# VectorE's expert loop cut to one head per pass, ScalarE's order in the memory stage, and chunk 1's output product finished ahead of its transpositions

## The chip, the cores and the metric

The kernel is one program on one core of a Trainium2 chip. The metric is the device time of one execution in microseconds (us); the number that counts is the median over the runs. TensorE (PE) multiplies matrices and transposes, VectorE (DVE), ScalarE (ACT) and GpSimd (POOL) work on tiles, and SyncE (SP) issues the ordinary loads. GpSimd issues the gathers. The engines run side by side and wait for each other through semaphores.

## The reference, cut to what matters

One layer over 256 tokens of width 1024, all in float32: a norm, one wide projection, then three branches (causal attention with rotary positions, a gated delta rule, and attention over 256 memory tokens), mixed by sigmoid gates and projected back; then a product-key expert layer.

```python
h = rms_norm(x, attn_norm_g); proj = h @ w_in
moba_out, dn_out = attention(8 heads), gated_delta_rule(8 heads) * silu(z)
mem_out = softmax(cq ck^T / 16) cv                     # 4 heads of 256
mixed = sum_n sigmoid(gate_n) * (branch_n @ w_branch[n])
x = x + mixed @ w_out
h2 = rms_norm(x, ffn_norm_g); q = h2 @ w_q             # 8 heads, two halves
experts, sc = top 16 of (top16(q1 keys1) + top16(q2 keys2))     # per token, per head
x = x + sum_k softmax(sc)_k * gelu(h2 . u[e_k]) * v[e_k]
```

The expert layer reads, for each of 256 tokens and 8 heads, 16 rows of 2048 floats (u and v of one expert lie side by side): 256 gathers of 1 MB.

## The kernel before

Each engine has its own program, written out by hand, and the order of that text is the order in which the engine works. Tokens are two chunks of 128 (c = 0, 1).

**Projection stages.** Weights come as tiles of 512 KB through a ring of three buffers (`raw` and `halves`, index i % 3). `load` (SP) fills `raw`, `high` (ACT, L555) writes a rounded copy, `low` (POOL, L918) the rest of it, and PE multiplies both (L1450 to L1452, 24 products a tile). `high` of a tile waits until PE is done with the tile three before it (`before`, `tiles_done`), `load` until that tile's `low` is done. The stages are "mv", "lead", "kv", seven times "head", "last", three times "mem", "mlast", "branch". While PE multiplies tiles, the small steps of a head lie between them: `fill(n)` puts n eighths of tiles ahead of the next small step.

**Memory stage.** `mem_head(m)` for m = 0 to 3. ACT turns the sums of squares into inverse roots (L769 to L775: Ln, then Exp), DVE scales query and key with them (L1195), PE makes the scores (L1708), ACT and DVE the softmax, PE turns it (L1715, event `p_turned`), ACT copies it out of PSUM (L558, `pT_ready`), and PE multiplies by the values (L1723). ACT also does for the next memory head: the copy of values (`take_mem_values`), squares and Silu of the delta rule's branch (`dn_head_squares`, L635 and L636), and at m = 0 the Sigmoid of the first eight gate tiles (L810). A change of function on ACT takes an ACT_TABLE_LOAD.

**Output and first routing.** PE makes `output(c, n)` (L1747, 16 pieces of products in two halves n), DVE adds it to x (`add_x1`, L1361), PE transposes it (`turn_x1`, L1756), DVE scales the transpose (`turned_x1`, L1367), and PE makes queries (L1762) and scores (L1769) of `first_head(c)`. DVE then finds the top 16 (`whole_route`). For chunk 1, DVE does in turn add_x1(1,0), turned_x1(1,0), add_x1(1,1), turned_x1(1,1), the norm and the routing, and only then its first expert row.

**Expert loop.** For each unit (head h, chunk c) GpSimd gathers 16 rows into a ring of 8 (`rows_uv`, L967); DVE takes the dot product with h2 (L1316), ACT the gelu (L859), DVE multiplies by the softmax weight (`coefficients`, L1324), ACT makes a diagonal matrix (L863), PE adds the row (L1799) and gives the ring slot back (`vrow`). Between its dots DVE routes the next head (`route_steps`). DVE's program has the bodies of heads 0 and 1 written out, a loop over j with two bodies (L1402, two passes: heads 2 to 5), and heads 6 and 7 written out. ACT and PE have a loop of two bodies with three passes (L907, L1837), GpSimd one unit pair a pass. The weights lie in four tiles `wts[par][c]`.

## Time and the profile before

| what | value |
|---|---|
| median of 3 runs | 1276.69 us (1274.66 to 1276.82) |
| profiled execution | 1273.94 us, its span 1272.1 us, mean clock 0.983 |
| PE busy | 1108.5 us, 87% of the span |
| DVE / ACT / POOL busy | 709.0 / 521.9 / 614.0 us |
| gathers | 268.45 MB of 355.32 MB moved |

The span runs from the first to the last instruction; 1.84 us of the profiled execution lie outside it. The profiled execution is 2.75 us faster than the median. Busy shares are means over stages with different limits, so they say little by themselves.

### The profile page before, as it was taken

How to read it: one execution, taken by the hardware profiler on the slowest of the kernel's cores; microseconds unless marked ns; L12 is line 12 of the kernel's file. 1: busy time of each engine (PE TensorE's matmuls, PEld its weight loads, DVE VectorE, ACT ScalarE, POOL GpSimd, SP SyncE). 2: the span in 40 equal slices, each digit the busy share in tenths (PEclk: the TensorE clock that was granted, in tenths of full speed). 3: DMA queues.
4: the chain of work that ended last, by engine and by line, in shares of the span. 5: the costliest groups of instructions: out<-in, count | busy, mean ns of one | idle time of the engine just before them, and what ended most of it. 6: DMA issues, size and time to landing. Idle time of an engine off the chain costs nothing.

```text
span 1272.1 us, 17107 instructions
## 1 busy us (share of the span) xinstructions
PE 1108.5 (87%) x5387; PEld 764.2 (60%) x5387; DVE 709.0 (56%) x1691; ACT 521.9 (41%) x1036; POOL 614.0 (48%) x447
## 2 busy tenths in 40 slices
PE   5989999999999999999888797797977978977776
PEld 5869999999998899885434252342523524422222
DVE  4535555554543332335766767666756666676554
ACT  4555566555565776512332223332333132321211
POOL 2376766567674666752234334343444434444331
PEclk8999999999999999999899999999989999999999
DMA  7453443343444453975799999999989999999996
GB/s 247 121 170 85 114 117 105 105 118 99 116 107 110 133 137 110 297 253 215 303 423 405 421 409 423 422 407 421 400 353 419 410 423 422 402 422 420 421 422 262
DMA packets 161377, 355.32 MB, mean 279 GB/s; under 512 B 7983, under 2 KB 123182, under 8 KB 127406
## 3 DMA queue, kind: packets, MB, share of 16 engines
q0 software_dynamic: 36864, 268.45, 51.3%
q1 hardware_dynamic: 124462, 86.27, 22.9%
q8 instruction: 22, 0.36, 0.1%
q14 instruction: 29, 0.24, 0.0%
HBM read 353.65 MB, written 1.05 MB: 279 GB/s over the span
## 4 chain that ended last, share of the span: by engine, by line
PE 49%; DMA 29%; issue 8%; ACT 6%; DVE 4%; POOL 4%; POOLq 0%; DVEq 0%; ACTq 0%; SPq 0%
DMA top<-peer_uv_dram,route 21%; PE ps L1799 13%; PE ps L1450 6%; PE ps L1451 6%; PE ps L1452 6%; DMA front<-peer_uv_dram,route 5%; PE ps L1762 4%; POOL split L918 2%; PE ps L1747 2%; PE ps L1610 2%; ACT split L555 2%; DMA front<-in_w_branch_dram 2%; PE ps L1629 2%; PE ps L1628 1%; ACT top L863 1%
## 5 line engine op out<-in xcount | busy, mean ns | idle before, releaser
L1799 PE MATMUL ps<-top 128*128 128x512 f32 x640 | 306.2, 619 | 91.6 <-ACT top L863 91.5
L918 POOL TENSOR_TENSOR split<-front,split 128x1024 fp32r<-128x1024 f32 x123 | 296.8, 2424 | 183.9 <-ACT split L555 183.7
L967 POOL DMA_INDIRECT top<-peer_uv_dram,route x160 | 166.0, 1038 | 261.0 <-PE ps L1799 253.5
L1799 PEld LDWEIGHTS ps<-top 128*128 128x128 f32 x640 | 118.8, 195 | 264.8 <-ACT top L863 149.7
L1316 DVE CUSTOM_DVE_ANT_0 top<-top,scratch 128x1024 f32<-128x1024 f32 x160 | 196.1, 1226 | 144.1 <-DMA top<-peer_uv_dram,route 144.1
L1450 PE MATMUL ps<-split 128*128 128x256 f32 (+1 forms) x768 | 241.4, 314 | 9.3 <-POOL split L918 5.0
L1451 PE MATMUL ps<-split 128*128 128x256 f32 (+1 forms) x768 | 225.1, 293 | 0.0
L1452 PE MATMUL ps<-split 128*128 128x256 f32 (+1 forms) x768 | 224.8, 293 | 0.0
L863 ACT ACTIVATE top<-cst,route 128x128 f32<-128x128 f32 x256 | 88.7, 393 | 280.9 <-DVE route L1324 277.5
L555 ACT ACTIVATE split<-front 128x1024 fp32r<-128x1024 f32 x128 | 133.7, 1056 | 140.6 <-PE ps L1452 85.9
L1450 PEld LDWEIGHTS ps<-split 128*128 128x128 f32 x768 | 147.1, 192 | 16.6 <-issue 8.4
L1799 PE MATMUL ps<-front,top 128*128 128x512 f32 x256 | 126.3, 617 | 34.9 <-ACT top L863 34.9
L1451 PEld LDWEIGHTS ps<-split 128*128 128x128 f32 x768 | 147.3, 192 | 3.8 <-issue 1.0
L1452 PEld LDWEIGHTS ps<-split 128*128 128x128 f32 x768 | 146.8, 191 | 2.9
L967 POOL DMA_INDIRECT front<-peer_uv_dram,route x64 | 66.9, 1045 | 136.4 <-PE ps L1799 94.6
L1799 PEld LDWEIGHTS ps<-front,top 128*128 128x128 f32 x256 | 47.7, 194 | 106.4 <-ACT top L863 55.0
L1316 DVE CUSTOM_DVE_ANT_0 front<-front,scratch 128x1024 f32<-128x1024 f32 x64 | 78.6, 1227 | 40.1 <-DMA front<-peer_uv_dram,route 32.8
L859 ACT ACTIVATE route<-route 128x2 f32<-128x2 f32 x128 | 26.0, 203 | 147.5 <-DVE route L1316 147.1
L1799 PE MATMUL ps<-scratch,top 128*128 128x512 f32 x128 | 61.0, 599 | 0.0
L1762 PE MATMUL ps<-scratch,branch_part 128*128 128x256 f32 (+1 forms) x288 | 58.5, 357 | 1.6 <-DVE scratch L1367 1.6
L1762 PEld LDWEIGHTS ps<-scratch,branch_part 128*128 128x128 f32 x288 | 50.2, 190 | 14.3 <-issue 7.2
L1450 PE MATMUL ps<-branch_hi,split 128*128 128x256 f32 x192 | 55.5, 289 | 1.5 <-POOL split L918 1.3
(263 smaller groups left out, 1594.3 us busy)
## 6 DMA issues: line engine op xcount, KB each, us to landing
front<-in_w_in_dram SPq DMA_DIRECT2D x88, 512.0 KB, 3.8
front<-in_w_branch_dram SPq DMA_DIRECT2D x24, 512.0 KB, 4.9
front<-in_w_mem_kv_dram SPq DMA_DIRECT2D x16, 512.0 KB, 3.9
top<-in_w_out_dram SPq DMA_DIRECT2D x8, 512.0 KB, 6.6
rest<-peer_w_q_by_head_dram SPq DMA_DIRECT2D x3, 1024.0 KB, 9.0
gate_part<-peer_w_q_by_head_dram SPq DMA_DIRECT2D x3, 1024.0 KB, 14.8
top<-peer_uv_dram,route POOLq DMA_INDIRECT x160, 10.3
branch_part<-peer_w_q_by_head_dram SPq DMA_DIRECT2D x2, 1024.0 KB, 6.1
```

The lines of the kernel that those rows point to most:

```text
L555: act.activation(halves[i % 3][:, 0], raw[i % 3], ACT.Copy).then_inc(hi_ready, 1)
L859: act.activation(gelu[c][:, a:b], acts[c][:, a:b], ACT.Gelu_apprx_tanh).then_inc(names["gelu"].sem, 1)
L863: act.activation(diag[:, k % 8, :], ident, ACT.Copy, scale=coef[c][:, k:k + 1]).then_inc(names["diag"].sem, 1)
L918: pool.tensor_tensor(halves[i % 3][:, 1], raw[i % 3], halves[i % 3][:, 0], ALU.subtract).then_inc(lo_ready, 1)
L967: pool.indirect_dma_start(rows_uv[k % RING], None, peer_uv, bass.IndirectOffsetOnAxis(ap=idx[c][:, k:k + 1], axis=0)).then_inc(s_row[k % R ...
L1316: dve.tensor_tensor_reduce(out=row, in0=row, in1=h2[:, c, :], scale=1.0, scalar=0.0, op0=ALU.mult, op1=ALU.add, accum_out=acts[c][:, k:k + ...
L1450: pe.matmul(dst, lhs[0], rhs[0], start=first, stop=False)
L1451: pe.matmul(dst, lhs[0], rhs[1], start=False, stop=False)
L1452: return pe.matmul(dst, lhs[1], rhs[0], start=False, stop=last)
L1610: ins = pe.matmul(ps[:, 4, a:b], BT[:, s, a:b], X[:, a:b], start=True, stop=True)
L1762: ins = pe.matmul(ps[:, 6 + i, a:b], wq[par][:, k, i * P:(i + 1) * P], h2T[:, k, a:b], start=(k == 0), stop=(k == KT - 1))
L1799: ins = pe.matmul(ps[:, 2 * c + half, :], diag[:, k % 8, :], rows_uv[k % RING][:, D + half * 512:D + (half + 1) * 512], start=False, stop= ...
```

## The change

It has four edits.

1. **DVE's expert loop.** The four weight tiles become one range, and `wts(par, c, a, b)` picks a part of it by an address that may hold a loop variable. Head 0 is written out, heads 1 to 6 are a loop in a loop (`j` and `par`) with one body, head 7 is written out. The parity of the heads is swapped.
2. **ACT ahead of the head loop.** The copies of `memv[0]` out of PSUM stand behind the first `high` of "head" and no longer behind the second.
3. **ACT in the memory stage.** The Sigmoid of gates 0 to 7 moves from memory head 0 into the last head, ahead of the wait for `dn_out`. `take_mem_values(0)` and the Silu `silu_z(0)` move behind the three `high` of memory head 0. The copy for `pT_ready` moves ahead of `high(tile 5)`, and in the last memory head ahead of the first "branch" `high` and the gate copy.
4. **PE.** `output(1, 1)` no longer has `turn_x1(1, 0)` between its sixth and seventh step; the transpositions follow it.

```diff
-        wts = [[small_of(TOPK) for _ in range(NC)] for _ in range(2)]
+        AT_WTS = at_route[0]
+        small_of(2 * NC * TOPK)
+        def wts(par, c, a=0, b=TOPK):
+            return route[:, bass.ds(par * (NC * TOPK) + (AT_WTS + c * TOPK + a), b - a)]
...
-            for i in range(2):
-                high("head", 0, i)
+            high("head", 0, 0)
             act.wait_ge(tiles_done, made("kv", 0, 7))
             for n in (1, 0):
                 act.activation(memv[0][:, n * 512:(n + 1) * 512], ps[:, 3 + n, :], ACT.Copy).then_inc(memv_kept, 1)
-            high("head", 0, 2)
+            for i in range(1, 3):
+                high("head", 0, i)
...
                 if last:
                     evacuate_mem(0, 1, kind)
+                    for gate in ("gate0", "gate1"):
+                        act.wait_ge(names[gate].sem, 1 + KT // 2)
+                    act.activation(gates[:, 0:8, :], gates[:, 0:8, :], ACT.Sigmoid).then_inc(names["sig"].sem, 1)
...
                 if last:
-                    act.wait_ge(names["vtok_kept"].sem, HEADS)
-                    take_mem_values(0)
                     dn_head_squares(0)
...
                 high(*of_head(h + 1, 1))
                 high(*of_head(h + 1, 2))
+                if last:
+                    act.wait_ge(names["vtok_kept"].sem, HEADS)
+                    take_mem_values(0)
+                    silu_z(0)
...
+                if not last:
+                    high(*tile(4))
+                    evacuate_mem(m + 1, 0, kind)
+                on(act, "p_turned", it)
+                copy("pT_ready", mpT, ps[:, 5, :])
                 if last:
                     high("branch", 0, 0)
                     act.wait_ge(tiles_done, made(*kind, 1))
                     copy("gate0", gates[:, 16 + 2 * m:18 + 2 * m, :], two(ps[:, 7, :]))
-                else:
-                    high(*tile(4))
-                    evacuate_mem(m + 1, 0, kind)
-                    high(*tile(5))
-                on(act, "p_turned", it)
-                copy("pT_ready", mpT, ps[:, 5, :])
...
-                    if m == 0:
-                        act.activation(gates[:, 0:8, :], gates[:, 0:8, :], ACT.Sigmoid).then_inc(names["sig"].sem, 1)
+                    silu_z(m + 1)
...
-            body_dve(0, 0, True, True)
-            body_dve(1, 1, True)
-            with dve.Fori(1, (PHEADS - 2) // 2) as j:
-                for par in range(2):
-                    body_dve(j * 2 + par, par, True)
-            body_dve(PHEADS - 2, 0, True)
-            body_dve(PHEADS - 1, 1, False)
+            body_dve(0, 1, True, True)
+            with dve.Fori(0, (PHEADS - 2) // 2) as j:
+                with dve.Fori(0, 2) as par:
+                    body_dve(j * 2 + par + 1, par, True)
+            body_dve(PHEADS - 1, 0, False)
...
-            output(1, 1, turn=(1, 0))
+            output(1, 1)
             pe.sem_inc(done("vrow"), PRIME)
+            turn_x1(1, 0)
             first_head(1)
```

On DVE, at the entry of the loop of the kernel before: the branch, and then the first rows of head 2. ISA rows of L1322 and L1323 are register steps, those of L1316 the dots.

```order
L1298 TENSOR_REDUCE route<-scratch 128x32
L1301 SCALAR_TENSOR_TENSOR route<-route 128x16
L1402 UNCONDITIONAL_BRANCH
L1402 ISA
L1316 ISA front,route<-front,scratch 128x1024
L1316 ISA route 128x1
L1322 ISA
L1323 ISA
L1324 TENSOR_TENSOR route<-route 128x2
```

The end of the new loop on DVE, with the two jumps back (L1414 the inner, L1413 the outer loop), followed by the first row of head 7.

```order
L1310 TENSOR_REDUCE route<-scratch 128x32
L1264 REGISTER_ALU
L1313 SCALAR_TENSOR_TENSOR route<-route 128x16
L1414 REGISTER_ALU
L1414 COMPARE_AND_BRANCH
L1413 REGISTER_ALU
L1413 COMPARE_AND_BRANCH
L1328 ISA front,route<-front,scratch 128x1024
```

In this listing the loop of before has 358 rows from its first to its jump, the new inner loop 197, ACT's loop (L907, the same before and now) 227. Each `coefficients` in the new loop has one register row more (of L1336) than before.

On ACT, from the last head into memory head 0, before: L558 of branch_part is `dn_kept`, the next two are `take_mem_values(0)`, L636 is the Silu, L555 the three `high` of memory head 0, L769 the start of the inverse roots.

```order
L558 ACTIVATE branch_part<-ps 128x256
L558 ACTIVATE scratch<-top 128x256
L558 ACTIVATE scratch<-memv 128x256
L635 ACTIVATE scratch<-branch_part 128x512
L636 ACT_TABLE_LOAD
L636 ACTIVATE scratch<-front 128x512
L558 ACTIVATE front<-ps 128x256
L558 ACTIVATE gate_part<-ps 128x256
L555 ACTIVATE split<-front 128x1024
L558 ACTIVATE gate_part<-ps 128x256
L555 ACTIVATE split<-front 128x1024 x2
L769 ACT_TABLE_LOAD
```

The same place on ACT of the changed kernel (L746 is the Sigmoid, L645 the Silu, L561 `high`; the row after these is L783, the former L769).

```order
L746 ACTIVATE gate_part<-gate_part 128x2048
L564 ACTIVATE branch_part<-ps 128x256
L641 ACTIVATE scratch<-branch_part 128x512
L564 ACTIVATE front<-ps 128x256
L564 ACTIVATE gate_part<-ps 128x256
L561 ACTIVATE split<-front 128x1024
L564 ACTIVATE gate_part<-ps 128x256
L561 ACTIVATE split<-front 128x1024 x2
L564 ACTIVATE scratch<-top 128x256
L564 ACTIVATE scratch<-memv 128x256
L645 ACT_TABLE_LOAD
L645 ACTIVATE scratch<-front 128x512
```

The two copies, the table load and the Silu stood ahead of the three `high` and now stand between them and the inverse roots.

On PE, chunk 1's output and first queries, before and then now (L1747/L1757 the output product, L1756/L1766 `turn_x1`, L1762/L1772 the queries).

```order
L1747 MATMUL ps<-top,front 128x512 x14
L1756 MATMUL ps<-cst,branch_part 128x128 x4
L1747 MATMUL ps<-top,front 128x512 x2
L1762 MATMUL ps<-scratch,branch_part 128x128 x8
L1756 MATMUL ps<-cst,branch_part 128x128 x4
```

```order
L1757 MATMUL ps<-top,front 128x512 x16
L1766 MATMUL ps<-cst,branch_part 128x128 x4
L1772 MATMUL ps<-scratch,branch_part 128x128 x8
L1766 MATMUL ps<-cst,branch_part 128x128 x4
```

The first four transpositions now stand directly ahead of the queries that need them.

## Rows read from the trace of the kernel before

**Rows 1.** The page, part 2: GB/s in 40 slices of 31.8 us.
```profile
GB/s 247 121 170 85 114 117 105 105 118 99 116 107 110 133 137 110 297 253 215 303 423 405 421 409 423 422 407 421 400 353 419 410 423 422 402 422 420 421 422 262
```

**Rows 2.** Chain that ended last: start us, us; first query of one head.
```profile
662.30 3.45 PE ps L1762 x16
...
905.99 3.45 PE ps L1762 x16
...
990.98 3.45 PE ps L1762 x16
```

**Rows 3.** Timeline of DVE at the end of head 3; idle time in brackets.
```profile
936.23 0.17 DVE L1301 SCALAR_TENSOR_TENSOR route<-route 128x16 uint32<-128x16 f32 x1
941.96 1.22 DVE L1316 CUSTOM_DVE_ANT_0 front<-front,scratch 128x1024 f32<-128x1024 f32 x1 [5.55 <-issue]
```

**Rows 4.** Line L1402, window 930 to 945: duration ns, first and last start us.
```profile
L1402 DVEq COMPARE_BRANCH  x1: 62/62/62, 936.3 to 936.3; - x1
L1402 DVEq FUSED_REGOPS  x1: 93/93/93, 941.8 to 941.8; - x1
```

**Rows 5.** Line L907, window 943 to 945: ACT's own jump back.
```profile
L907 ACTq COMPARE_BRANCH  x1: 45/45/45, 943.7 to 943.7; - x1
L907 ACTq FUSED_REGOPS  x1: 68/68/68, 943.9 to 943.9; - x1
```

**Rows 6.** Timelines of DVE, ACT and PE ahead of the head loop.
```profile
90.91 1.29 DVE L1183 COPY memv<-ps 128x512 f32<-128x512 f32 x2 [11.06 <-PE ps L1452]
...
92.07 1.06 ACT L555 ACTIVATE split<-front 128x1024 fp32r<-128x1024 f32 x1 [2.50 <-DMA front<-in_w_in_dram]
93.03 1.07 ACT L703 ACTIVATE top<-ps 128x512 f32<-128x512 f32 x2
...
94.44 1.10 PE L1585 MATMUL ps<-rest 128*128 128x512 f32 x2 [3.56 <-ACT top L703]
```

**Rows 7.** Timelines of ACT, PE and DVE, last head into memory head 0.
```profile
396.15 0.39 ACT L558 ACTIVATE branch_part<-ps 128x256 f32<-128x256 f32 x1 [6.43 <-PE ps L1650]
396.43 0.41 ACT L558 ACTIVATE scratch<-top 128x256 f32<-128x256 f32 x1
...
397.68 1.28 ACT L636 ACT_TABLE_LOAD   x1
...
399.51 0.37 ACT L558 ACTIVATE front<-ps 128x256 f32<-128x256 f32 x1
...
403.28 1.28 ACT L769 ACT_TABLE_LOAD   x1
...
399.19 1.89 PE L1695 MATMUL ps<-scratch,cst 128*128 128x256 f32 x8
...
407.82 1.52 DVE L1195 TENSOR_TENSOR scratch<-scratch 128x1024 f32<-128x1024 f32 x1 [12.68 <-ACT scratch L773]
```

**Rows 8.** Chain that ended last: memory head 0's scores.
```profile
409.66 1.74 PE ps L1708 x8
```

**Rows 9.** PE's waits, 395 to 565 us: us in total, times, longest.
```profile
PE ps L1723 <- ACT scratch L558: 4.2, 4, 2.1
```

**Rows 10.** Timeline of PE: the start of memory head 1, and of "branch".
```profile
436.10 0.39 PE L1450 MATMUL ps<-split 128*128 128x256 f32 x1 [1.67 <-POOL split L918]
...
514.96 0.47 PE L1450 MATMUL ps<-branch_hi,split 128*128 128x256 f32 x1
```

**Rows 11.** Timeline of ACT: `high` of the fourth "branch" tile, after the Sigmoids.
```profile
519.08 1.04 ACT L555 ACTIVATE split<-front 128x1024 fp32r<-128x1024 f32 x1
```

**Rows 12.** Chain that ended last: output and first queries of chunk 1.
```profile
596.77 0.44 PE ps L1756 x4
597.21 1.72 PE ps L1747 x4
...
601.18 0.70 DVE scratch L1367
```

**Rows 13.** Timeline of POOL: the ninth gather.
```profile
624.42 1.12 POOL L967 DMA_INDIRECT front<-peer_uv_dram,route  x1 [18.50 <-PE ps L1799]
```

More of the change, by code:

```diff
@@ L635, in dn_head_squares, with silu_z @@
                 act.activation(two(sqd), branch[:, 8 + 2 * m:10 + 2 * m, :], ACT.Square).then_inc(names["dn_sq"].sem, 1)
+            def silu_z(m):
                 act.activation(two(zs), zT[:, 2 * m:2 * m + 2, :], ACT.Silu).then_inc(names["z_silu"].sem, 1)
@@ L790, in mem_head @@
                     copy("gate0", gates[:, 16 + 2 * m:18 + 2 * m, :], two(ps[:, 7, :]))
-                else:
-                    high(*tile(4))
-                    evacuate_mem(m + 1, 0, kind)
-                    high(*tile(5))
-                on(act, "p_turned", it)
-                copy("pT_ready", mpT, ps[:, 5, :])
-                if last:
                     high("branch", 0, 1)
@@ L800, in mem_head @@
                 else:
+                    high(*tile(5))
                     high(*tile(6))
@@ L1303, in route_steps, with weigh @@
                 assert step[0] == RSTEPS
-            def weigh(n, out):
+            def weigh(n, par, c):
                 on(dve, "exps", n)
@@ L1309, in weigh @@
                 dve.wait_ge(done("weighed"), n * 2 + 1)
-                dve.tensor_scalar(out, ex, rsum[:, 0:1], None, ALU.mult).then_inc(done("weighed"), 1)
+                dve.tensor_scalar(wts(par, c), ex, rsum[:, 0:1], None, ALU.mult).then_inc(done("weighed"), 1)
             def dot(n, c, k):
@@ L1323, in coefficients @@
                 dve.wait_ge(done("gelu"), n * NG + (g + 1))
-                dve.tensor_tensor(coef[c][:, a:b], gelu[c][:, a:b], weights[:, a:b], ALU.mult).then_inc(done("coef"), 1)
+                dve.tensor_tensor(coef[c][:, a:b], gelu[c][:, a:b], wts(weights, c, a, b), ALU.mult).then_inc(done("coef"), 1)
             def add_out(c):
@@ L1332, in unit_dve @@
             def unit_dve(n, c, par, steps, first=False, last=False):
-                before_w, after_w = (wts[par][0], wts[1 - par][0]) if c else (wts[1 - par][1], wts[par][1])
+                other = par * -1 + 1
                 for k in range(TOPK):
@@ L1338, in unit_dve @@
                     if k == 0 and not first:
-                        coefficients(n - 1, 1 - c, NG - 1, before_w)
+                        coefficients(n - 1, 1 - c, NG - 1, par if c else other)
                     elif k and k % GROUP == 0:
-                        coefficients(n, c, k // GROUP - 1, wts[par][c])
+                        coefficients(n, c, k // GROUP - 1, par)
                     if k == 7 and not first and not last:
-                        weigh(n + 1, after_w)
+                        weigh(n + 1, other if c else par, 1 - c)
                     if k == 12 and last:
@@ L1394, in _ @@
             norm_dve(1)
-            weigh(0, wts[0][0])
+            weigh(0, 1, 0)
             whole_route(1, 1)
-            weigh(1, wts[0][1])
+            weigh(1, 1, 1)
             for c in range(NC):
                 dve.wait_ge(t_h2[c], 4)
-            body_dve(0, 0, True, True)
-            body_dve(1, 1, True)
-            with dve.Fori(1, (PHEADS - 2) // 2) as j:
-                for par in range(2):
-                    body_dve(j * 2 + par, par, True)
-            body_dve(PHEADS - 2, 0, True)
-            body_dve(PHEADS - 1, 1, False)
-            coefficients(UNITS - 1, 1, NG - 1, wts[1][1])
+            body_dve(0, 1, True, True)
[3 more added lines that the diff above has]
+            body_dve(PHEADS - 1, 0, False)
+            coefficients(UNITS - 1, 1, NG - 1, 0)
             add_out(1)
```

## The prediction, on record before the run

> **What bounds the kernel now.** I read the bytes moved per slice first. Up to slice 16 the rates are mostly between 85 and 250 GB/s, and PE has hardly a pause there. From slice 21 on they stay at about 420 GB/s, with one slice at 353 [rows 1]. So there are two regimes. Up to about 560 us PE sets the time, and only what ends one of its waits can count. In the expert loop the gathers set it, and only what leaves them without work counts. Between the two, from 565 to 620 us, lies a chain through PE, DVE and ACT that neither hides.
>
> In the loop I used the chain of waits as a clock. The first query product of a head starts at 662.30, 905.99 and 990.98 us (heads 0, 3 and 4) [rows 2]. The three heads up to 905.99 take 243.69, which is 81.23 each. The next takes 84.99, 3.76 more. The timeline of DVE shows why: after the last row of head 3's routing it stands idle for 5.55 us, and nothing released it ("issue") [rows 3]. The line view names the place: the jump back of L1402 is issued at 936.3, and the first instruction at its target only at 941.8 [rows 4]. Neither a semaphore nor a row was missing. The instructions themselves were. The slice at 353 GB/s is the same place.
>
> **Edit 1, the loop on DVE.** It removes that jump's stall and puts five jumps back in its place (three inner, two outer). The question is what each costs. The old loop has 358 rows in the listing, the new one 197. The nearest row is ACT's loop of 227 rows: its jump back is issued at 943.7, its target at 943.9 [rows 5], so 0.2 us for a body longer than the new one. I take that, and count it as nothing, since DVE has slack at every row while the gathers run at full rate. The added register row in each coefficient step (at most 0.1 us each, by the 93 ns of such a step in [rows 4]) is covered the same way. If that cover were gone, 16 of them would add up to 1.5 us a head. What the stall costs is not its 5.55 us, since the ring of eight rows carries some of it, but the 3.76 us by which that head is longer. The bounds are 3 (the heads differ by half a microsecond among themselves) and 5.5. **Term: -3.7 us.**
>
> The Trainium skill has a rule that speaks against this edit (Runtime: NRT & Kernel Launch, section on instruction fetch mechanics): instructions are fetched in order in blocks of 16 KiB or 256 instructions, two of them are held, and a taken branch out of that window waits for a fetch. By it the new body, close to a block long and lying across two, would have its start dropped for the block ahead, and every jump back would stall. By it ACT's jump in [rows 5] should have stalled too, and it did not, so I give this rule the small chance of the first rival and let the row decide. By the rule the sum at the end would be 1288.1 us, by the row 1269.6.
>
> **Edit 2, ahead of the head loop.** PE sat idle for 3.56 us and was released at 94.44 by ACT's copies L703. These came at 93.03 because a `high` stood ahead of them, and that one had waited for its load until 92.07 [rows 6]. Now the copies can start when PE is done with "kv". DVE's twin copies show when: at 90.91, done at 92.20. So ACT ends near 92.0 and the `high` starts at 92.07 or just after. It is not late next, since its load sets it. PE is released by DVE's copies at about 92.5. The first GpSimd pieces gain only 1 us, but they have a microsecond of slack. The bounds are 0.9 and 2.1. **Term: -1.9 us**, kept to the end since PE has no wait in the heads that follow.
>
> **Edit 3, the memory stage, in the order of time.** The Sigmoid (a table load and a pass, 3.2 us of ACT) moves into a stretch in which ACT waits for `dn_out` for 6.43 us [rows 7], so there it costs nothing. Behind it, two copies, table load and Silu leave the way of the three `high`. From the first copy at 396.43 they took 0.6 us, and from 397.68 to 399.51 1.8 us [rows 7]. But the first `high` needs the buffer of the last tile of "last", and PE starts what follows that tile only at 399.19 [rows 7]. It gains some 0.7 us, not 2.4. The 2.4 us now stand behind the third `high`, in front of the inverse roots (403.28), which start 1.8 us later. DVE's scaling L1195 (407.82, done at 409.34) follows them at once, and PE's scores at 409.66 [rows 8] had only 0.3 us to spare. What is late next are the scores: **+1.6 us**.
>
> In return, three things. (a) PE waited for `pT_ready` four times, 4.2 us together, of which the last is 2.1 [rows 9]. The copy now comes ahead of a `high` of 1 us, which ends the three short waits (2.1 us together). In memory head 0 I count only 0.1 of its 0.6, since its fifth tile's `low` is delayed with the scores: **-1.6 us**. The long one, in the last head, ends too, but the next tile at 514.96 [rows 10] needs a `high` and a `low` that can start only when PE has freed a buffer, as before: **-0.15 us**. (b) Without the Sigmoid between them, the `high` of memory head 1 come 3.2 us earlier, and PE's wait of 1.67 us at 436.10 [rows 10] goes: **-1.65 us**. (c) In the last head, the two last Sigmoids and the `high` at 519.08 [rows 11] come up to 0.9 us earlier, and with them the chain of loads of the "branch" stage, every third tile. The loads there share the engines with those of w_out, so I take **-0.6 us** out of 0 to 0.9. The sum of edit 3 is +1.6 - 1.6 - 0.15 - 1.65 - 0.6 = **-2.4 us**. Its bounds are +1.6 (nothing but the delay) and -6 (no delay, all waits gone).
>
> **Edit 4, PE's output.** Before, the four transpositions (0.44 us, 596.77 to 597.21) came ahead of the last 1.72 us of the product, and DVE's copy of 0.70 us [rows 12] ran under that product. Now they come after it, and both the first queries and DVE's next step (add_x1(1,1), 0.7 us, queued behind that copy) wait for the copy: output 0.44 earlier, then transpositions, then a bare copy. The queries start at 0.70 plus hand-overs of 0.06 later, and once PE has stopped, the pass takes up to 0.25 longer. Behind it follow the second transposition, the norm, the routing and the first dot. The ring is full by then and POOL's ninth gather waits 18.50 us for the first slot [rows 13], so nothing hides it. **Term: +0.9 us**, bounds +0.6 and +1.2. A gain would need DVE's addition to go ahead of its copy, and the text of DVE is unchanged.
>
> **Sum.** -3.7 - 1.9 - 2.4 + 0.9 = -7.1 us. The profiled execution would go from 1273.94 to 1266.8. It lies 2.75 us under the median of before, and I carry the change over to the median: 1276.69 - 7.1 = **1269.6 us**.
>
> **Rivals.**
> 1. *Every jump back of the new loop stalls* (slower). The place is L1414 and L1413, the price 3.7 us each, 18.5 for five. The time is 1276.7 - 7.1 + 18.5 = 1288.1 us. It decides the sign from two stalled jumps on (7.4 against 7.1). For it: one jump back did stall. Against it: ACT's longer loop did not, at 943.7. Chance 0.05.
> 2. *The memory stage gives nothing back.* The delay of the scores stays, and the waits for `pT_ready` turn into waits for tiles, since each tile's way (load, `high`, `low`) also follows ACT. Edit 3 is then +1.6, the sum -3.1, the time 1273.6. For it: in head 0 that is what I find. Against it: memory heads 1 and 2 have tiles ready ahead. Chance 0.12.
> 3. *The whole memory stage pays.* The inverse roots are not late, since the `high` come 2.4 us earlier after all. Edit 3 is -6, the sum -10.7, the time 1266.0. Against it stands the buffer that PE frees at 399.19. Chance 0.10.
> 4. *Edits 3 and 4 go wrong together with a smaller loop term*, no change: some -2 us, 1274.7. Chance 0.07.
>
> The forecast itself has 0.66.
>
> **How the numbers follow.** The forecast's own range takes -3.0 to -5.5 for the loop and -0.9 to -2.1 for the head start, with the memory stage between -0.5 and -4, which gives about 1267 to 1272.5. Rivals 2 and 3 widen it to 1265.5 and 1273.8, and these leave out rival 1, most of rival 4 and a little on either side. A measurement of this kernel can tell 0.2% (2.6 us) from no change: faster means under 1274.1. Faster: the forecast, rivals 2 and 3 nearly whole, 0.87. Same 0.07. Slower 0.06.
>
> **What would show it.** Loop: no idle time over 1 us on DVE at a jump, six nearly equal heads of 81 us on PE, and no slice under 400 GB/s within the loop. Five waits of 5 us at L1413 and L1414 would prove rival 1. Head start: PE's L1585 (now L1595 or so) near 92.5. Memory: the first scores come later by about 1.6 us relative to the end of the last head, with a wait of some 2 us ended by DVE ahead of them; no wait for `pT_ready`; no wait at the start of memory head 1. If the first scores are not late, rival 3 holds. Output: from the end of chunk 0's scores to DVE's first dot 0.9 us more than before, with a new wait of PE ahead of the first queries of chunk 1.

## The result and the profile after

The changed kernel runs in 1262.99 us (median of 4, 1261.43 to 1269.24), the kernel before on the same chip in 1276.76 (median of 4): ratio 0.9907, 95% interval 0.9888 to 0.9926. Forecast were 1269.6 us and a range from 1265.5 to 1273.8. The direction was right; the gain is twice as large as said and lies outside the range. The profiled execution took 1261.72 us, its span went from 1272.1 to 1259.7 us.

The page of the changed kernel, parts 1 to 3, answers to [rows 1]. No slice of the expert loop (from the 21st on) is under 400 GB/s now, the last, part-filled one left out.

```profile
span 1259.7 us, 17302 instructions
...
GB/s 245 123 167 111 99 128 104 101 117 100 117 102 117 133 136 102 286 249 218 286 421 416 422 417 411 422 420 421 422 415 421 415 422 422 407 422 421 422 421 279
...
q14 instruction: 18, 0.15, 0.0%
```

In part 3 of the page of before the last line reads:

```profile
q14 instruction: 29, 0.24, 0.0%
```

These are packets of 8 KB by which engines fetch their own code, 29 before, 18 now. I had not looked at this line.

The chain that ended last, changed kernel: the first query product of each of six heads (answers to [rows 2]). The distances are 81.4, 79.5, 80.4, 79.8 and 80.7 us. Three whole heads of before had taken 81.23 each.

```profile
659.99 3.45 PE ps L1772 x16
...
741.40 3.45 PE ps L1772 x16
...
820.88 3.45 PE ps L1772 x16
...
901.30 3.45 PE ps L1772 x16
...
981.05 3.45 PE ps L1772 x16
...
1061.71 3.45 PE ps L1772 x16
```

One jump back of the new loop: its line, window 925 to 935 (answers to [rows 4, 5]), and DVE's timeline there (answers to [rows 3]). The jump is issued at 930.3, its target at 930.6. The product behind it starts at 930.92, ended by a row and not by "issue".

```profile
L1414 DVEq COMPARE_BRANCH  x1: 56/56/56, 930.3 to 930.3; - x1
L1414 DVEq FUSED_REGOPS  x1: 204/204/204, 930.6 to 930.6; - x1
```

```profile
930.92 1.23 DVE L1328 CUSTOM_DVE_ANT_0 front<-front,scratch 128x1024 f32<-128x1024 f32 x1 [0.49 <-DMA front<-peer_uv_dram,route]
```

The timeline of PE, changed kernel, at the other places of the prediction (answers to [rows 6, 8, 10, 12]), and of DVE at its first row product:

```profile
92.72 1.10 PE L1595 MATMUL ps<-rest 128*128 128x512 f32 x2 [1.81 <-DVE memv L1195]
...
408.18 1.99 PE L1718 MATMUL ps<-scratch 128*128 128x256 f32 x8 [1.99 <-DVE scratch L1207]
...
440.55 0.70 PE L1718 MATMUL ps<-scratch 128*128 128x256 f32 x2 [1.27 <-DVE scratch L1207]
...
511.56 0.36 PE L1460 MATMUL ps<-branch_hi,split 128*128 128x256 f32 x1 [1.94 <-POOL split L930]
...
596.84 1.35 PE L1772 MATMUL ps<-scratch,branch_part 128*128 128x128 f32 x10 [0.87 <-DVE scratch L1379]
...
614.20 1.23 DVE L1328 CUSTOM_DVE_ANT_0 front<-front,scratch 128x1024 f32<-128x1024 f32 x1
```

The time came in three stretches. Up to the end of the head loop (DVE's last branch there, 360.82 us before, 357.92 now) 2.9 us. Up to the first output product (564.17, now 561.22) nothing more. From there to DVE's first row product (its dot product with one gathered row; 616.04, now 614.20) 1.1 us were given back. From the first to the last row product, 645.87 us before and 635.17 now, 10.7 us were gained. That last one is the surprise: 3.7 was forecast.

### The profile page after: what moved, and what is told of

Read it like the earlier page. It is cut to its first block, busy times and chain, and to the rows that moved or that the text cites. A ratio compares the mean times of both kernels' runs of the same rounds, so it can differ in the third digit from the quotient of the medians.

```text
span 1259.7 us, 17302 instructions
## 1 busy us (share of the span) xinstructions
PE 1100.6 (87%) x5387; PEld 761.8 (60%) x5387; DVE 703.7 (56%) x1691; ACT 522.4 (41%) x1036; POOL 614.4 (49%) x447
## 4 chain that ended last, share of the span: by engine, by line
PE 54%; DMA 28%; issue 7%; ACT 4%; DVE 3%; POOL 3%; DVEq 0%; POOLq 0%; ACTq 0%; SPq 0%
DMA top<-peer_uv_dram,route 23%; PE ps L1809 12%; PE ps L1460 8%; PE ps L1461 8%; PE ps L1462 8%; PE ps L1772 4%; DMA front<-peer_uv_dram,route 3%; PE ps L1757 2%; POOL split L930 2%; PE ps L1620 2%; DMA front<-in_w_branch_dram 2%; PE ps L1639 2%; PE ps L1638 2%; ACT split L561 1%; ACT top L875 1%
## 5 line engine op out<-in xcount | busy, mean ns | idle before, releaser
L1809 PE MATMUL ps<-top 128*128 128x512 f32 x640 | 300.8, 609 | 90.2 <-ACT top L875 90.1
L561 ACT ACTIVATE split<-front 128x1024 fp32r<-128x1024 f32 x128 | 133.5, 1056 | 144.4 <-PE ps L1462 85.8
L979 POOL DMA_INDIRECT front<-peer_uv_dram,route x64 | 66.6, 1040 | 131.7 <-PE ps L1809 87.5
L1772 PE MATMUL ps<-scratch,branch_part 128*128 128x256 f32 (+1 forms) x288 | 58.5, 357 | 2.4 <-DVE scratch L1379 2.4
L1772 PEld LDWEIGHTS ps<-scratch,branch_part 128*128 128x128 f32 x288 | 50.1, 190 | 14.9 <-issue 7.8
```

The source lines that it names most:

```text
L561: act.activation(halves[i % 3][:, 0], raw[i % 3], ACT.Copy).then_inc(hi_ready, 1)
L979: pool.indirect_dma_start(rows_uv[k % RING], None, peer_uv, bass.IndirectOffsetOnAxis(ap=idx[c][:, k:k + 1], axis=0)).then_inc(s_row[k % R ...
L1772: ins = pe.matmul(ps[:, 6 + i, a:b], wq[par][:, k, i * P:(i + 1) * P], h2T[:, k, a:b], start=(k == 0), stop=(k == KT - 1))
L1809: ins = pe.matmul(ps[:, 2 * c + half, :], diag[:, k % 8, :], rows_uv[k % RING][:, D + half * 512:D + (half + 1) * 512], start=False, stop= ...
```

## The experiments

The eleven runs were made on three other chips: A had `loop_alone`, `dve_unrolled`, `act_pool_unrolled` and `output_undone`, B had `after_again`, `unrolled_padded`, `loop_padded` and `best`, C had `loop_undone`, `start_alone` and `memory_alone`. The kernel before took 1280.87, 1279.89 and 1279.55 us on A, B and C, 3 to 4 us more than in the first pair. So kernel times are given as ratios to the kernel before on the same chip. A stretch is read from the one trace of a run, and where two chips are compared the text says so. What the first two traces show stood behind the runs. In the loop of before every 17 to 18 products one comes 3.4 us after the one ahead, not 2.49, and in the same microsecond the records show one 8 KB fetch of code. The timeline of DVE, kernel before, and the DMA view of its window 839 to 843 us:

```profile
838.84 1.23 DVE L1316 CUSTOM_DVE_ANT_0 top<-top,scratch 128x1024 f32<-128x1024 f32 x1 [0.46 <-DMA top<-peer_uv_dram,route]
...
842.29 1.23 DVE L1316 CUSTOM_DVE_ANT_0 top<-top,scratch 128x1024 f32<-128x1024 f32 x1 [1.80 <-DMA top<-peer_uv_dram,route]
...
844.78 1.23 DVE L1316 CUSTOM_DVE_ANT_0 top<-top,scratch 128x1024 f32<-128x1024 f32 x1 [0.84 <-DMA top<-peer_uv_dram,route]
```

```profile
q0 software_dynamic: 189, 1.35, 96.3%
q14 instruction: 1, 0.01, 0.5%
```

**Edit 1 alone** (`loop_alone`: the kernel before with the hunks on `wts`, `weigh`, `coefficients`, `unit_dve` and the loop).

```diff
-            with dve.Fori(1, (PHEADS - 2) // 2) as j:
-                for par in range(2):
-                    body_dve(j * 2 + par, par, True)
+            with dve.Fori(0, (PHEADS - 2) // 2) as j:
+                with dve.Fori(0, 2) as par:
+                    body_dve(j * 2 + par + 1, par, True)
```

> The kernel before with edit 1 alone (VectorE's loop of one head). Measured is the stretch from DVE's first to its last row product, 645.87 us before and 635.17 after, 256 rows. Theory A (code fetches): each fetch of an 8 KB block of instructions, 19 between 630 and 1240 us before and 8 after, delays the gathered row in flight by up to 1 us, and this is paid where the ring runs empty; with the 3.7 us of the stall that makes 10.7. It expects 635 to 636 us here, and a kernel time of 1266 to 1267 us. Theory B (the stall is worth more than 3.76 us, nothing else counts) expects the same stretch. Theory C (the stretch of before was long by chance, or owes its end to the other edits' earlier start) expects 642 us, the 3.7 of the prediction, and 1273 us.

Measured: 0.9946 (0.9926 to 0.9966), which is 6.9 us, and 641.63 us from first to last product. The kernel time falls between the theories, the stretch is theory C's by this one trace. The runs below give the spread that I lacked here.

**The six heads written out** (`dve_unrolled`).

```diff
-            with dve.Fori(0, (PHEADS - 2) // 2) as j:
-                with dve.Fori(0, 2) as par:
-                    body_dve(j * 2 + par + 1, par, True)
+            for h in range(1, PHEADS - 1):
+                body_dve(h, (h + 1) % 2, True)
```

> The changed kernel with VectorE's six loop heads written out one after the other: no jump and no stall, but its code is read through once, so that the fetches of 8 KB in the stretch rise from 8 to about 18, as many as before. Theory A (a fetch costs about 0.65 us each, 7 us for 11 of them) expects 641 to 643 us from first to last row product and a kernel time near 1270 us. Theory B (only the stall costs) expects 635 us and 1263 us. This is the run that tells them apart.

Measured: 0.9923 (0.9908 to 0.9938), 640.82 us. No jump and no stall, but 3 us more from first to last product than in the two runs of the same chip that keep the new loop (`act_pool_unrolled` and `output_undone` below: 637.91 and 637.39 us), and a median of 1270.37 us against their 1268.10 and 1268.30. Theory B is out. Theory A has the sign right and the size wrong: it counted on some 18 fetches and 7 us. The trace has 15 in the stretch, seven more than with the new loop, and 2.9 to 3.4 us. The table below shows why: the new loop loses 2.7 to 6.4 us at the head boundaries beside its fetches, this kernel 0.8, at one row. The timeline of DVE shows the delay itself as in before, at a fetch at 801.20:

```profile
799.84 1.22 DVE L1328 CUSTOM_DVE_ANT_0 top<-top,scratch 128x1024 f32<-128x1024 f32 x1 [0.47 <-DMA top<-peer_uv_dram,route]
...
803.29 1.23 DVE L1328 CUSTOM_DVE_ANT_0 top<-top,scratch 128x1024 f32<-128x1024 f32 x1 [1.80 <-DMA top<-peer_uv_dram,route]
...
805.77 1.23 DVE L1328 CUSTOM_DVE_ANT_0 top<-top,scratch 128x1024 f32<-128x1024 f32 x1 [0.84 <-DMA top<-peer_uv_dram,route]
```

**The loops of ACT and POOL written out** (`act_pool_unrolled`; DVE's code as in the changed kernel).

```diff
-            with act.Fori(0, (PHEADS - 2) // 2) as j:
-                for par in range(2):
-                    body_act(j * 2 + par, True, True, j, par)
+            for h in range(PHEADS - 2):
+                body_act(h, True, True, h // 2, h % 2)
...
-            with pool.Fori(1, PHEADS) as h:
+            for h in range(1, PHEADS):
```

> The changed kernel with the expert loops of ScalarE and GpSimd written out: VectorE's code as after, but about ten more fetches of 8 KB by the other two engines. Theory A in its form 'any fetch takes room from the gathers' expects 640 to 642 us from first to last row product, 1269 us in all. In its form 'only VectorE's fetches count, since they hold up its own products' it expects 635 us and 1263 us, and so does theory B.

Measured: 0.9905 (0.9890 to 0.9920), 637.91 us: no slower than the changed kernel within the intervals (0.9897 on chip B; `output_undone`, on the same chip, has 0.9908). The timeline of DVE around a fetch by one of the two others at 970.43, and the DMA view of 969 to 973 us. The rows keep their 2.49 us.

```profile
970.41 1.23 DVE L1327 CUSTOM_DVE_ANT_0 front<-front,scratch 128x1024 f32<-128x1024 f32 x1 [0.93 <-DMA front<-peer_uv_dram,route]
972.90 1.23 DVE L1327 CUSTOM_DVE_ANT_0 top<-top,scratch 128x1024 f32<-128x1024 f32 x1 [0.65 <-DMA top<-peer_uv_dram,route]
```

```profile
q14 instruction: 1, 0.01, 0.5%
```

The records of single packets say more. A gathered packet of 8 KB mostly takes 309 to 325 ns. The one that starts when a fetch has ended takes longer, and by a different amount for the two sorts (three of each: start of the fetch in us, the packet behind it in ns):

```
before              795.75 968    840.20 968    883.72 969
dve_unrolled        801.20 968    854.27 968    909.88 968
act_pool_unrolled   970.43 687   1017.14 662   1095.72 655
```

Take the two packets as one after the other on the same one of the 16 DMA engines (the records name no engine). Then it loses 0.32 + 0.97 - 0.31 = 0.98 us at a fetch of DVE, and the row of that moment is 0.93 to 0.97 us late. At a fetch of the others it loses 0.66 to 0.69. At 970.43 no row is late, and at the other two, near head boundaries, the rows are no later than in traces without such a fetch.

**Longer code, written out and in the loop** (`unrolled_padded`, `loop_padded`), the same edit in both:

```diff
                     dot(n, c, k)
+                    if steps is not None:
+                        for _ in range(4):
+                            dve.wait_ge(s_gain, 16)
```

> VectorE's six heads written out as in dve_unrolled, and four waits that are long fulfilled ahead of every row product, so that a head's code is longer by 128 instructions: about one fetch of 8 KB more per head, some 3 instead of 2. Theory A (0.93 us per fetch) expects six or seven more rows of 3.4 us, and 645.5 to 647.5 us from first to last row product, against 640.8 in dve_unrolled; kernel time near 1276 us. The rival (a fetch costs only while something else is late, and padding is hidden by VectorE's slack at every row) expects 641 us and 1270.5 us.

Measured: 0.9950 (0.9932 to 0.9969), 645.57 us, 4.75 more than without the padding (chip A). The waits stand behind each dot, and came out two to an instruction, so a head grew by 64 instructions and not by 128. The late rows now come every 16 products and not every 21. The stretch has 19 fetches and not 15, so 1.2 us for each of the four more, with whatever else differs between the two traces. The rival is out. In the middle of heads 1 to 5, with two fetches each, the excess is 1.7 to 1.9 us, twice 0.93. In head 6 it is 1.4: one of its two fetches made a row only 0.5 us late.

> The changed kernel, its loop of one head, with the same four fulfilled waits ahead of every row product: the body grows from 249 to about 377 instructions. If what is held of the code ends between 265 (no stall) and 462 instructions (one stall of 5.5 us), this shows on which side 377 lies. Theory 'holds it' expects no fetch inside the loop and the time of the changed kernel, up to 1 us more. Theory 'too long' expects every head to fetch its code anew, two to three fetches a head at 0.93 us, and a stall at each of the jumps back at 3.7 us: 25 us more.

Measured: 0.9989 (0.9975 to 1.0003), 652.97 us, 15 more than the changed kernel here. The body is 313 recorded instructions (249 without the padding). Its inner jump back, over 313, costs 0.2 us. The outer one, over 317, stalls. The lines of the two loops, window 850 to 1040, and DVE's timeline:

```profile
L1416 DVEq COMPARE_BRANCH  x2: 63/65/67, 857.9 to 1026.1; - x2
L1416 DVEq MOVE  x2: 43/43/43, 864.8 to 1033.2; - x2
```

```profile
1033.64 1.23 DVE L1328 CUSTOM_DVE_ANT_0 front<-front,scratch 128x1024 f32<-128x1024 f32 x1 [8.03 <-issue]
```

The jumps of 857.9 and 1026.1 reach their target at 864.8 and 1033.2: 6.9 and 7.1 us. Neither theory had this: the body as such is held, and one that starts four instructions earlier is not. A code that starts elsewhere in its blocks may come out otherwise; that was not tried.

**The changed kernel again, and without edit 1** (`after_again`, `loop_undone`; the latter is `loop_alone`'s edit taken back).

> The changed kernel itself, once more, as the partner of the three runs beside it. Theory A (each fetch of VectorE's own code costs a row 0.93 us, the other engines' nothing) expects what its first profile showed: 0.0 us above 20 times the median row in the middle of heads 2 to 7, 0.9 only where a fetch of VectorE falls. The head boundaries, without a fetch, have given anything from 0 to 1.7 us; the stretch from first to last row product should lie at 635 to 638 us. If it lies near 645 the first profile was luck.

> The changed kernel with edit 1 undone: VectorE's old loop of two heads, all other edits kept. The prediction's own terms for the rest are -3.4 us (0.9973 of before). From the first traces, first row product 1.84 us earlier and the loop's stretch as in before, 645.9 us, theory A expects 0.9985 of before. From the run with edit 1 alone (0.9946) and the changed kernel (0.9897) on one chip the rest should be worth 0.9951. The trace should show the ten rows of 3.4 us at fetches of VectorE and one stall of about 5.5 us again.

Measured: 0.9897 (0.9878 to 0.9916) with 638.11 us, and 0.9975 (0.9964 to 0.9986) with 646.70 us. Each ratio is to the kernel before on its own chip. By them edit 1 is worth 0.9897 / 0.9975, 10 us beside the other edits, and 6.9 alone; the intervals allow the two to be the same. The prediction's 0.9973 for the other edits lies inside the interval of `loop_undone`, the 0.9951 worked out from `loop_alone` does not. The stall is back in `loop_undone`, with 5.71 us. The ten late rows are not all back: of its eight fetches of DVE in heads 2 to 7 away from the stall, six are followed by a row 0.7 to 1.0 us late, and those at 1100.67 and 1155.02 us by none. Together with the other traces:

```
                          first to last   middle of   boundaries  chip
                          product, us     7 heads     (6)
old loop   before           645.87          6.3          7.4      first
           loop_undone      646.70          6.1          7.7      C
           start_alone      649.03          6.1         10.0      C
           memory_alone     644.91          6.4          7.2      C
new loop   after            635.17          0.7          3.5      first
           after_again      638.11          1.0          4.4      B
           output_undone    637.39          0.2          4.7      A
           best             639.21          1.5          4.6      B
           loop_alone       641.63          1.7          6.4      A
written    dve_unrolled     640.82          4.6          3.6      A
out        unrolled_padded  645.57         11.6          1.0      B
```

The last two columns are worked out from the starts of the row products: what the 20 intervals from product 6 to 26 of a head (heads 1 to 7), and the 12 from there to product 6 of the next (heads 1 to 6), take above 2.486 us each. The old loop means 646.6 us, the new one 638.3: 8.3 us, with 5.2 in the middles and 3.4 at the boundaries (the rest of the stretch takes 0.3 back). The middles are the cleaner measure: in heads 2 to 7 they are 0.0 or 0.1 in every trace of the new loop.

How regular is the delay? In the six traces of the old loop and the written-out code DVE has 51 fetches in heads 2 to 7, the four around each stall left out. Behind 44 of them a row is 0.7 to 1.0 us late (once 2.4), behind four of them 0.4 to 0.6 us, and behind three hardly at all. One of these three, in `dve_unrolled`, is the fetch at 1122.10, and DVE's timeline there:

```profile
1121.90 1.22 DVE L1328 CUSTOM_DVE_ANT_0 scratch<-scratch 128x1024 f32<-128x1024 f32 x1 [0.84 <-DMA scratch<-peer_uv_dram,route]
...
1124.49 1.23 DVE L1328 CUSTOM_DVE_ANT_0 top<-top,scratch 128x1024 f32<-128x1024 f32 x1 [0.56 <-DMA top<-peer_uv_dram,route]
```

What spared these rows is not shown.

**Edits 2 and 3 alone, and edit 4 undone** (`start_alone`, `memory_alone`: the kernel before with the hunks of that edit; `output_undone`: the changed kernel with this edit).

```diff
-            output(1, 1)
+            output(1, 1, turn=(1, 0))
             pe.sem_inc(done("vrow"), PRIME)
-            turn_x1(1, 0)
```

> The kernel before with edit 2 alone (two copies ahead of the second high). Predicted -1.9 us at the end of the head loop, bounds 0.9 and 2.1; the changed kernel's trace had 2.9 there, of which 0.86 is a wait of PE at 101 us that is gone. If edit 2 alone does both, PE reaches the end of the head loop 2.9 us earlier and keeps it to the expert loop; if the 0.86 came with the memory edits it shows 1.7 to 2.0.

> The kernel before with edit 3 alone (ScalarE's order in the memory stage). Predicted -2.4 us, bounds +1.6 and -6. The changed kernel's trace gives, after edit 2's 2.9 us are taken off, +1.6 at the first memory scores and -0.5 at the first tile of the branch stage. Theory D (the wait of 1.67 us at the start of memory head 1 only moves, to that head's scores) expects -0.5 here too: memory head 0's scores 1.6 us later than in before, memory head 1's scores still 1.5 later, the branch stage's first tile 0.5 us earlier.

> The changed kernel with edit 4 undone (chunk 1's transpositions again between the two parts of its output product). The prediction's term is 0.9 us: from the end of the second chunk's output product to DVE's first row product 0.9 us less than in the changed kernel, first row product near 613.3 instead of 614.2 us, and a kernel time 0.9 us lower, 1262.1. The rival, that the gathers do not start their steady stream sooner since their ring is full, expects the first product earlier but no change of the time.

Measured: 0.9974 (0.9957 to 0.9991), 1.0008 (0.9993 to 1.0022) and 0.9908 (0.9893 to 0.9922). The times at which five points are reached, against `loop_alone` (chip A), whose program is that of before up to there; differences in us (scores of memory heads 0, 1, 3 and first output product on PE):

```
                 head loop ends  scores 0   scores 1   scores 3   output
loop_alone       362.25          410.89     443.04     504.22     565.48
start_alone       -3.2            -2.7       -0.3       -1.6       -1.1
memory_alone      -0.3            +1.9       +3.2       +1.3       +1.1
after_again       -3.1            -1.1       -1.2       -3.1       -3.4
```

The two do not add up: -1.1 and +1.1 alone, -3.4 together. What stands between may be PE's clock. Two windows views, `memory_alone` behind its wait of 2.00 us ahead of the first scores, and `loop_alone` behind the wait of 3.57 us that edit 2 shortens (us, busy time of the engines, then the granted clock):

```profile
410.00:413.00 3.00, 1.00 (x8) 0.80 (x7) 1.50 (x2) 2.99 (x4) 0.00 (x0) 1.00 0.64 181
413.00:417.00 4.00, 4.00 (x15) 3.48 (x15) 2.20 (x4) 2.25 (x3) 2.19 (x1) 0.57 0.00 0
```

```profile
93.00:100.00 7.00, 5.66 (x17) 4.19 (x18) 1.82 (x5) 2.44 (x5) 4.52 (x5) 0.52 0.55 154
```

The clock fell to 1.2 GHz for some 3.4 us in the first case, of which at most half is lost, and for nearly all of the 7 us in the second. `start_alone` shows the same behind a wait of 1.96 us at the start of memory head 1 (0.83 over 430 to 440 us). The changed kernel has a wait of the same 2 us ahead of its first scores, and no such fall there in two traces. Of the nine traces with this wait, `memory_alone` and `loop_padded` have the fall. Whether a wait of 2 us draws one differs from run to run.

If the falls in `start_alone` and `memory_alone` cost 1.7 us each, the two edits alone would be -2.8 and -0.6, and add up to the -3.4. But `loop_padded`, with its fall at 409 us (0.63 over 408 to 412), reaches the first output product 202.7 us after the end of the head loop, and the seven others with the same program up to there take 202.6 to 203.5. So a fall need not cost anything, and that the clock is the cause here is argued, not shown. That distance also measures edit 3: it is 203.35 in before and 203.23 in `loop_alone`, and 203.04 in the mean of these eight traces, 0.3 us less.

`output_undone` reaches the first row product 55.29 us after the first output product, `after_again` after 55.16. That looks like no difference, but the two ran on different chips. In all six traces with the old order of PE, chunk 1's first queries start 34.59 us after the first output product, and in all seven with the new order 35.62 or 35.63, 1.0 us later. `after_again` has a wait there as the changed kernel's first trace has:

```profile
597.71 2.02 PE L1772 MATMUL ps<-scratch,branch_part 128*128 128x128 f32 x16 [0.88 <-DVE scratch L1379]
```

From the first output product to the first row product the traces have, in us:

```
chip    old order of PE                              new order of PE
first   51.87 (before)                               52.98 (after)
A       55.29 (output_undone), 55.90 (loop_alone)    55.32, 55.54
B       53.99 (best)                                 55.13, 55.13, 55.16
C       53.94, 53.94 (start_, memory_alone)          55.46 (loop_undone)
```

So edit 4 costs 1.1 to 1.5 us on three of the four chips, and nothing on A. What hides it there is ACT's copy of the queries (L856). It starts 0.04 us after PE's last query product in the first pair, 1.5 to 1.9 us after it on B, C and in the new order on A, and 3.0 us after it in the two traces of the old order on A, for nothing in the program that the trace names. In `output_undone`:

```profile
605.46 0.38 ACT L856 ACTIVATE scratch<-ps 128x256 f32<-128x256 f32 x1 [4.76 <-remote]
```

**A version from the findings** (`best`): the changed kernel with edit 4 undone, and the Silu moved into ACT's idle time.

```diff
                 copy("gate0", gates[:, bass.ds(h * 2, 1), :], ps[:, 7, None, T:HT])
+                if last:
+                    silu_z(0)
                 high(*of_head(h + 1, 0))
...
                     take_mem_values(0)
-                    silu_z(0)
```

> The changed kernel with edit 4 undone, and in the last head ScalarE's Silu of memory head 0 put into the idle time of 1.78 us ahead of the first of the three high, the two value copies left behind them. From the trace of the changed kernel: the inverse roots start some 1.8 us earlier, PE's wait of 1.99 us ahead of memory head 0's scores nearly goes (theory: 1.8 us of it), and with 1.1 us from edit 4 the first row product comes at 611.3 us, 2.9 earlier than in the changed kernel. The rival: the next tile's low and high are late instead (a wait of 1 us moves behind the scores), and only 1.1 to 1.9 us remain.

Measured: 0.9879 (0.9860 to 0.9897), against 0.9897 (0.9878 to 0.9916) for the changed kernel beside it. That is no sure difference. The first row product comes at 614.53 us, 2.7 earlier than in `after_again`, but 1.5 of that is there at the end of the head loop already, and 1.2 is edit 4 undone (53.99 against 55.16 us). That it comes near the 2.9 expected is luck: the 1.8 us expected from the earlier inverse roots came to nothing. PE's wait ahead of the first scores is gone, and the branch stage starts 2.0 us earlier relative to the end of the head loop. The output product starts at the same distance from it (202.9 us in both). PE's waits from 500 to 562 us, `best` first, then `after_again`: the gain went into waits for tiles.

```profile
PE ps L1461 <- POOL split L931: 5.0, 4, 1.9
```

```profile
PE ps L1460 <- POOL split L930: 3.4, 3, 1.9
```

## Why the prediction was wrong, step by step

**The loop: "Term: -3.7 us".** This is the step that failed: -10.7 in the first pair of traces, -8.3 between the means of four and five, so some of the first pair's gain may be the spread of single traces (635.17 to 641.63 us with the new loop). The price of the stall itself was right. The boundary where it fell has 4.3 us of excess in before and 0.2 after, and 3.4 lie between the means of four and five. What I missed is that the long body cost something at nearly every one of its blocks, too. DVE's loop of 462 instructions was read anew all the time. From head 1 to head 7 the table has 6.3 + 7.4 = 13.7 us of excess for before: nine fetches with a row 0.5 to 1.0 us late behind each, about 8, the boundary with the stall (and a tenth fetch), 4.3, and 1.4 of other things, of which 0.9 is the eighth row behind the stall. (The fetch at 962.32, right behind that row, made none late.) The changed kernel has 4.2: two fetches, at the rows 48 and 97, 1.6, and 2.6 at boundaries without one. That is 9.5 of the 10.7; the rest lies in head 0 and the last rows. I had read the 81.23 us of a head as what a head takes. 32 rows of 2.486 are 79.55, and the difference was in the rows all along.

That DVE's fetches cause the late rows is shown by the two written-out runs: in the middles the rows come where fetches come, move with their distance (17.5, 21 and 16 products) and are missing without them, though seven of the 51 fetches cost less or nothing. The rows at the boundaries are another matter, and stay open. Why only DVE's fetches do it is argued, not shown: the engine that serves them may be the one that ends a row anyway, and another has room for 0.68 us. The records don't name the engine.

**The five jumps counted as nothing** held as far as the jumps go: 0.2 to 0.4 us each at the jump itself, and a product that is late by 0.6 to 0.9 us behind an outer jump is followed by one that is early by as much. The Trainium skill (Runtime: NRT & Kernel Launch, Instruction fetch mechanics) says that a taken branch out of the window of two blocks forces a fetch. The trace agrees that there is such a window, by the stalls over 462 and 317 instructions, but bodies of 249, 265 (ACT) and 313 came back without a stall. It also calls the cost of crossing a block mostly hidden and full unrolling preferable; here a crossing on DVE mostly cost 0.93 us, and on chip A the written-out loop took 1270.37 us where the loop took 1268.10 and 1268.30.

**The head start: "-1.9 us"** was too small: -2.9. The wait fell from 3.56 to 1.81 as worked out, and PE's start at 92.72 is the forecast "near 92.5". But a second wait of 0.86 us at 101 us, that I had not looked for behind the first, ended too. In `loop_alone`, whose program is that of before up to there, this wait is missing and the clock was at 1.2 GHz for nearly 7 us. The size is not firm: in the ten traces with edit 2 the head loop ends at 357.65 to 359.60 us, 1.2 to 3.2 before the 360.82 of the kernel before.

**The memory stage: "-2.4 us"** was wrong in its sum: 0.0 in the first pair, -0.3 from `after_again` less edit 2 and in the mean of eight traces, no gain alone. Its first item was right. The first scores came 1.6 us later relative to the end of the head loop, behind a wait of 1.99 us ended by DVE. (b), the 1.67 us at the start of memory head 1, failed: the wait is gone, but 1.27 us stand ahead of that head's scores instead, and they are as late as the first. This is rival 2's mechanism in one place. (a), the waits for `pT_ready`, paid: 0.97 and 0.94 us in the next two heads. So the branch stage started 0.5 us earlier relative to the end of the head loop, and that was gone at the first output product. (c), the 0.6 us of the branch stage, did not come in this pair. In the changed kernel's trace the 1.94 us ahead of the branch stage were followed by 3.4 us at 1.2 GHz (0.57 over 512 to 516 us), but `after_again`, without this fall, gained only 0.4 us more on the same way.

**Edit 4: "+0.9 us"** was right: +1.1 in the first pair, with the wait ahead of the first queries, 0.87, that was named, and 1.1 to 1.5 on chips B and C. On chip A it cost nothing, since ACT's copy was later in the old order too.

**The sum.** -2.9 + 0.0 + 1.1 - 10.7 = -12.5, against -12.4 in the spans. The errors of edits 2 and 3 are of opposite sign and cancel to 1.4, which is luck; the loop alone took the time out of the range. The range of the forecast itself, 1267 to 1272.5, was also narrower than its own terms: their ends add up to -10.7 and -3.5 us, 1266.0 and 1273.2.

## What to carry to other kernels

In a stage bound by transfers at full rate, the length of an engine's loop can have a price per block of code and not only per jump, as DVE's had here. Count the instruction fetches in part 3 of the page and look for rows that come late at equal distances before pricing a loop by its stall. Compare the period of a pass with the sum of its parts at the median rate: 81.23 against 79.55 would have shown beforehand that each head lost 1.7 us somewhere. And a wait moved along a chain of `high` and `low` is paid only where the chain is not the bound: look at the next consumer too, as at memory head 1's scores.

## What the runs showed of the hardware

- By the packets behind three of each, a fetch of 8 KB of DVE's code held one DMA engine for 0.98 us among gathers at 420 GB/s, three times its own 0.32 us; one of ACT's or POOL's 0.66 to 0.69 us. Behind 44 of 51 fetches of DVE a row came 0.7 us late or more.
- DVE's jump back over 313 instructions took 0.2 us, one over 317 in the same program 6.9 and 7.1 us, one over 462 in before 5.5 us.
- After waits of PE of 1.9 to 3.6 us the granted clock was at 1.2 GHz for 3.4 us or nearly 7 us in some executions and not in others of the same program (behind 1.94 us in `after`, 0.57 over 512 to 516 us, and not in `after_again`, 1.00).
- What stays open: the excess at head boundaries of the new loop (0.0 to 1.8 us each, 2.7 to 6.4 us in all beside fetches, about 0.3 in before but 2 us more in `loop_undone` and `start_alone`), the seven fetches of DVE that cost less, and ACT's late copy at L856, 1.5 of the 2.2 us (52.98 and 55.16) by which the changed kernel's way from output to first row product differs between the first chip and B.
